# Dilated attention: softmax statistics of three groups joined over HBM instead of on TensorE

## The chip, the cores and the metric

The kernel runs on one NeuronCore of a Trainium2 chip. The metric is the device time of one execution in microseconds (us). Three executions of the kernel before took 3893.87 us in the median (3893.62 to 3896.42). A measurement of this kernel can tell a change of about 0.2% (some 8 us) from no change.

## The reference, cut to what matters

Two blocks of two layers each run over 512 tokens of width 1024, in float32. Only the last mixer, dilated attention in the second block, is touched. It has 16 heads of width 64 and three groups: group 0 with dilation 1, group 1 with dilation 4, group 2 with dilation 16. Each group has its own queries, keys and values. The three results are joined by their log-sum-exp:

```python
for g, (window, dilation) in enumerate(DIL_GROUPS):      # ((128, 1), (512, 4), (2048, 16))
    o, lse = strided_window_attention(q[g], k[g], v[g], dilation, window // dilation, rel_bias[g])
alpha = jax.nn.softmax(jnp.stack(lses, axis=0), axis=0)
o = jnp.sum(alpha[..., None] * jnp.stack(outs, axis=0), axis=0)
return o.reshape(B, S, DIL_WIDTH) @ w_o
```

For a token and a head that is one softmax over the keys of all three groups: the largest logit of the three is taken off before the exponential, and the three sums of exponentials are added.

## The kernel before, in words

All activations stay in SBUF with channels on the partitions and the 512 tokens on the free axis. Every linear layer is a chain of matmuls: a weight tile 128x128 is split into a high part `whi` and a low part `wlo`, the activations into `HH` and `HL`, and three matmuls (L409, L410, L411) make each product. The weights come from HBM in blocks of 8 tiles. SyncE (SP) loads a block 4 blocks ahead (`feed`, `load`), ScalarE (ACT) makes `whi`, VectorE (DVE) makes `wlo`. Each engine has its own program, written out by hand in order, and each wait is on a named signal. Nothing is rearranged by a scheduler.

The dilated stage (`dilated` in each engine's program) works in 8 rounds `c`, one for each pair of heads `hh_` = 0 and 1. A round has 9 steps. In step `n` TensorE (PE) first runs `head_proj(c + 1, n)`, the 24 matmuls of one of the nine projections (q, k, v of three groups) of the next pair, and after each v projection four transposes (L737). Then it runs `attend(c, n)`, a piece of the attention of this pair. The other engines run the same 9 steps: first their part of the projection, then their part of the attention. In the last round, `c` = 7, there is no projection left to put between the pieces.

The softmax statistics of a pair lie as columns: 12 tiles `s` (4 of each group) with 128 queries on the partitions, in `cm` (maxima), `cn` (negated joint maxima) and `cs` (sums). The queries of a tile are in the order of their group: in group 1 the tokens 4i + r, in group 2 the tokens of four residues of 16. To join the groups, their values must stand in token order. The pieces are:

- steps 0, 1: `logits`, q times k (L748 group 0, L755 group 1, L763 group 2). q and k lie in token order, so groups 1 and 2 are read with a stride of 4 or 16 elements. DVE adds the bias and takes the maxima (`biased`, L2032).
- step 2: `max_rows`, 12 matmuls turn the maxima to rows in token order (L777). DVE takes the maximum of three rows (`mrow`, L2043 to L2047).
- step 3: `max_cols`, 24 small matmuls turn the row back to 12 columns (L787, L790). DVE negates them (L2054).
- step 4, ACT only: `exps`, 24 exponentials with their sums, both heads (L1336).
- step 5: `sum_rows` adds the sums of the groups on PE (L798), DVE inverts them (L2060). Then `values` of head 0: 12 transposes of the exponentials (L808), ACT copies them to `PD` (`probs`, L1347), DVE spreads group 2 (`spread_probs`, L2067), PE multiplies by the values (L818, L824, L830).
- step 6: `values` of head 1.
- step 7: `spread` copies the inverse sums to 64 partitions each (L837), ACT takes them to `T[0]` (L1356), DVE multiplies (`finish`, L2073).

After round 7 comes the output projection `out_proj("dil")`, eight chains `m` of 24 matmuls. Each needs the results of all eight pairs, pair 7 at its end.

Of the kernel before, what the change touches and what calls it, by code (L numbers as in the profile page):

```python
# [16 lines left out]
S = 512  # L17
P = 128
# [81 lines left out]
def const_arrays():  # L100
# [11 lines left out]
    sel = np.zeros((P, P))  # L112
    sel[0, :64] = 1.0
    sel[1, 64:] = 1.0
    c["sel"] = sel
# [12 lines left out]
                ("band", 256), ("adiag", 4), ("sel", 128)]  # L128
# [76 lines left out]
def program(nc, xt, wst, mst, crow, vec, cst, trig, oh, tab, wax, out, bvec):  # L205
    with ExitStack() as ctx:
# [111 lines left out]
        mrow = at("mrow", cb_off + 2048, [2, S])  # L318
        cm = small[:, 64:88].rearrange("p (j h) -> p j h", h=2)
        cn = small[:, 88:112].rearrange("p (j h) -> p j h", h=2)  # L320
        cs = small[:, 112:136].rearrange("p (j h) -> p j h", h=2)
# [8 lines left out]
        def tok_view(ap, g, j):  # L330
            if g == 0:
                return ap[:, 128 * j:128 * j + 128]
            if g == 1:
                return ap.rearrange("p (i r) -> p r i", r=4)[:, j, :]
            return ap.rearrange("p (k a j) -> p j a k", k=32, a=4)[:, j, :, :]
# [19 lines left out]
            Signal(sem(n), 16) for n in ("vec_in", "cb_in", "wax_in", "oh_in", "tab_in", "trig_in", "fv_out", "x_out"))  # L355
        bb_in = [Signal(sem("bb_in%d" % i), 16) for i in range(2)]
# [3 lines left out]
        signals += x_in + [vec_in, cb_in, wax_in, oh_in, tab_in, trig_in, fv_out, x_out]  # L360

# [20 lines left out]
        def tensor_engine(lane):  # L382
# [341 lines left out]
            def dilated():  # L724
# [4 lines left out]
                def head_proj(c, n):  # L729
                    if c or n >= 4:  # L730
                        proj([("dl", c, n)], 8, hh, hl, ready)
                    g = n // 3
                    if n % 3 == 2:
                        o = take(("vt", c, g), main[0])
                        lane.wait_ge(a_mix, ("vt", c, g))
                        for j in range(4):
                            ins = e.transpose(o[:, 128 * j:128 * j + 128], tok_view(VT[:, g, :], g % 2, j), C["ident"][:])  # L737
                        ins.then_inc(*mm_done.up(("vt", c, g)))

                def logits(c, hh_):  # L740
# [19 lines left out]
                    for a_ in range(4):  # L760
                        for j in range(4):
                            r = 4 * a_ + j
                            ins = e.matmul(o[3][32 * j:32 * j + 32, 32 * a_:32 * a_ + 32], qk[hs, 4, r:S:16], qk[hs, 5, r:S:16],  # L763
                                           start=True, stop=True)
                    ins.then_inc(*mm_done.up(("lg", c, hh_, 3)))

                def row_view(o, g, j):
                    if g == 2:
                        return o.rearrange("p (i a j) -> p a j i", i=32, a=4)[:, j, :, :]
                    return tok_view(o, g, j)  # L770

                def max_rows(c):
                    o = take(("cm", c), pool_b)
                    lane.wait_ge(v_mix, ("lg", c, 1, 3))
                    for s in range(12):
                        g, j = s // 4, s % 4
                        ins = e.matmul(row_view(o[32 * g:32 * g + 2, :], g, j), cm[:, s, :], C["ident"][:], start=True, stop=True)  # L777
                    ins.then_inc(*mm_done.up(("cm", c)))

                def max_cols(c):  # L780
                    o = take(("cn", c), pool_b)
                    lane.wait_ge(v_mix, ("mrow", c))
                    for s in range(12):
                        g, j = s // 4, s % 4
                        at_ = o[:, 2 * s:2 * s + 2]
                        if g < 2:
                            e.matmul(at_, tok_view(mrow[:], g, j), C["ident"][0:2, 0:2], start=True, stop=True)  # L787
                            continue
                        for z in range(4):
                            ins = e.matmul(at_[32 * z:32 * z + 32, :], mrow[:, 4 * j + z:S:16], C["ident"][0:2, 0:2],  # L790
                                           start=True, stop=True)
                    ins.then_inc(*mm_done.up(("cn", c)))

                def sum_rows(c):
                    o = take(("cs", c), pool_b)
                    lane.wait_ge(a_mix, ("ex", c, 1))
                    for s in range(12):
                        ins = e.matmul(row_view(o[0:2, :], s // 4, s % 4), cs[:, s, :], C["ident"][:],  # L798
                                       start=s == 0, stop=s == 11, skip_group_check=True)
                    ins.then_inc(*mm_done.up(("cs", c)))  # L800

                def values(c, hh_):
# [26 lines left out]
                    for j in range(4):  # L829
                        ins = e.matmul(oh_.rearrange("p (i a j) -> p j a i", i=32, a=4)[:, j, :, :], vn[:, 8 + j, fs],  # L830
# [3 lines left out]
                def spread(c):  # L834
                    o = take(("sel", c), pool_b)
                    lane.wait_ge(v_mix, ("rc", c))
                    e.matmul(o, C["sel"][0:2, :], mrow[:], start=True, stop=True).then_inc(*mm_done.up(("sel", c)))  # L837
# [53 lines left out]
            lane.wait_ge(c_in["sel"], "in")  # L891
# [6 lines left out]
        def scalar_engine(lane):  # L898
# [406 lines left out]
            def dilated():  # L1305
                feed(8)

                def head_proj(c, n):
# [3 lines left out]
                    if n % 3 == 0:  # L1312
# [3 lines left out]
                        e.activation(QK[c % 2][:, 2 * g, :], bank(key), ACT.Copy, scale=0.125).then_inc(*a_mix.up(("dq", c, g)))  # L1316
                        freed[key] = ((a_mix, ("dq", c, g)),)
                    elif n % 3 == 2:
                        dst, src = VT[:, g, :], bank(key)
                        if g == 2:  # L1320
                            dst = dst.rearrange("p (j a k) -> p j a k", j=4, a=4)
                            src = src.rearrange("p (k a j) -> p j a k", k=32, a=4)
# [6 lines left out]
                def exps(c):  # L1329
                    lane.wait_ge(v_mix, ("cn", c))  # L1330
                    if c:
                        lane.wait_ge(mm_done, ("cs", c - 1))
                    for hh_ in range(2):
                        for s in range(12):
                            dst = SD[hh_][:, sd_at[s]:sd_at[s] + sd_wid[s]]
                            ins = e.activation(dst, dst, ACT.Exp, bias=cn[:, s, hh_:hh_ + 1], accum_out=cs[:, s, hh_:hh_ + 1])  # L1336
# [1142 lines left out]
```

## Time and profile before

| what | value |
|---|---|
| median of three runs | 3893.87 us |
| the profiled execution: its own time / its span | 3898.84 us / 3897.1 us |
| mean granted TensorE clock (1.00 is 2.4 GHz, 0.50 is 1.2 GHz) | 0.962 |
| PE busy / DVE busy / ACT busy | 3697.7 us (95%) / 2048.0 us (53%) / 1338.6 us (34%) |
| DMA share over the span | 31.0% of 16 engines |
| dilated stage, first logits to the last piece of round 7 | 2815.7 to 3455.9 us |

The trace gives each instruction's start and length. A busy PE row holds several matmuls, and neighbours overlap a little in it because matmuls are pipelined; a float32 matmul stands in it as two records. "Idle before" with an arrow names the instruction that ended the wait.

### The profile page before, as it was taken

To read this page: it belongs to the slowest core of one execution; us is meant where nothing else is said; L and a number is where in the kernel's file an instruction comes from. 1 tells how busy PE (TensorE), PEld (TensorE's weight loads), DVE (VectorE), ACT (ScalarE), POOL (GpSimd) and SP (SyncE) were. 2 spreads that over 40 slices of the span, in tenths; PEclk is the share of its full clock that TensorE was granted. 3 is DMA by queue.
4 is the path that set the end of the run, shared out by engine and by line. 5 is a ranking of instruction groups with operands and counts; after the bars stand their busy time and mean duration, and the time that the engine had idled before them with its cause. 6 is when DMAs were issued, how large, how long until landed. Compare 5 with 4: busy or idle time off the path is not lost.

```text
span 3897.1 us, 42188 instructions
## 1 busy us (share of the span) xinstructions
PE 3697.7 (95%) x17108; PEld 2932.7 (75%) x17108; DVE 2048.0 (53%) x3576; ACT 1338.6 (34%) x2299; POOL 127.9 (3%) x126
## 2 busy tenths in 40 slices
PE   6889999899999999988999999999999999989998
PEld 4647888666888788866678887888777777767886
DVE  7856756676756654466663246334533333345234
ACT  3563323443323322334432233223222322233222
POOL 2330000000000000001100000000000000000000
PEclk9999999989999999989999999999999999989999
DMA  6214555313555455311022222223211121112221
GB/s 243 97 44 164 203 185 189 140 56 119 185 202 189 170 195 193 110 66 38 20 78 98 97 98 81 98 93 100 82 59 59 59 65 63 55 44 87 96 94 65
DMA packets 125023, 426.58 MB, mean 109 GB/s; under 512 B 16107, under 2 KB 21099, under 8 KB 124828
## 3 DMA queue, kind: packets, MB, share of 16 engines
q1 hardware_dynamic: 124828, 423.88, 31.0%
q8 instruction: 135, 2.21, 0.2%
q14 instruction: 60, 0.49, 0.0%
HBM read 421.68 MB, written 2.14 MB: 109 GB/s over the span
## 4 chain that ended last, share of the span: by engine, by line
PE 84%; DVE 11%; ACT 3%; issue 1%; POOL 0%; ACTq 0%; DVEq 0%; POOLq 0%
PE ps L409 24%; PE ps L410 24%; PE ps L411 24%; PE ps L708 1%; PE ps L453 1%; PE ps L755 1%; PE ps L748 1%; PE ps L446 1%; DVE mrow L2060 1%; DVE TT L1522 1%; DVE HL L1507 1%; DVE wlo L1455 1%; PE ps L798 1%; PE ps L787 1%; DVE X L1608 1%
## 5 line engine op out<-in xcount | busy, mean ns | idle before, releaser
L409 PE MATMUL ps<-HH,whi 128*128 128x512 f32 x3168 | 1271.7, 401 | 45.3 <-DVE HL L1507 27.0
L410 PE MATMUL ps<-HL,whi 128*128 128x512 f32 x3168 | 1253.1, 396 | 0.0
L411 PE MATMUL ps<-HH,wlo 128*128 128x512 f32 x3168 | 1250.8, 395 | 0.0
L1455 DVE TENSOR_TENSOR wlo<-wraw,whi 128x1024 fp32r<-128x1024 f32 x526 | 643.8, 1224 | 692.0 <-ACT whi L920 691.8
L920 ACT ACTIVATE whi<-wraw 128x1024 fp32r<-128x1024 f32 x548 | 576.3, 1054 | 636.1 <-PE ps L411 624.2
L409 PEld LDWEIGHTS ps<-HH,whi 128*128 128x128 f32 x3168 | 607.0, 192 | 209.0 <-issue 67.2
L411 PEld LDWEIGHTS ps<-HH,wlo 128*128 128x128 f32 x3168 | 606.4, 191 | 130.4
L410 PEld LDWEIGHTS ps<-HL,whi 128*128 128x128 f32 x3168 | 607.2, 192 | 128.9 <-issue 4.6
L1443 DVE CUSTOM_DVE_ANT_0 mraw<-mraw,CB 128x1024 f32<-128x1024 f32 x224 | 282.3, 1261 | 0.8 <-DMA mraw<-mst 0.7
L1641 DVE TENSOR_TENSOR TT<-TT,ps 128x512 f32<-128x512 f32 x116 | 79.7, 687 | 217.2 <-PE ps L411 186.4
L409 PE MATMUL ps<-PHf,whi 128*128 128x512 f32 x352 | 136.9, 389 | 0.0
L410 PE MATMUL ps<-PLf,whi 128*128 128x512 f32 x352 | 136.9, 389 | 0.0
L409 PE MATMUL ps<-PHa,whi 128*128 128x512 f32 x352 | 136.9, 389 | 0.0
L410 PE MATMUL ps<-PLa,whi 128*128 128x512 f32 x352 | 136.9, 389 | 0.0
L409 PE MATMUL ps<-PHb,whi 128*128 128x512 f32 x352 | 136.9, 389 | 0.0
L410 PE MATMUL ps<-PLb,whi 128*128 128x512 f32 x352 | 136.9, 389 | 0.0
L411 PE MATMUL ps<-PHf,wlo 128*128 128x512 f32 x352 | 136.9, 389 | 0.0
L411 PE MATMUL ps<-PHa,wlo 128*128 128x512 f32 x352 | 136.9, 389 | 0.0
L411 PE MATMUL ps<-PHb,wlo 128*128 128x512 f32 x352 | 136.9, 389 | 0.0
L997 ACT ACTIVATE TT<-ps 128x512 f32<-128x512 f32 x72 | 42.9, 596 | 234.1 <-PE ps L411 234.1
L963 ACT ACTIVATE HH<-TT,MOD 128x512 fp32r<-128x512 f32 x63 | 45.2, 723 | 145.1 <-DVE TT L1522 145.1
L1336 ACT ACTIVATE SD<-SD,small 128x128 f32<-128x128 f32 (+1 forms) x192 | 74.1, 387 | 35.4 <-DVE small L2054 35.4
(329 smaller groups left out, 4012.5 us busy)
## 6 DMA issues: line engine op xcount, KB each, us to landing
wraw<-wst SPq DMA_DIRECT2D x548, 512.0 KB, 3.4
mraw<-mst SPq DMA_DIRECT2D x224, 512.0 KB, 3.4
MR<-mst SPq DMA_DIRECT2D x16, 512.0 KB, 13.8
X<-xt SPq DMA_DIRECT2D x8, 256.0 KB, 5.1
BB<-bvec SPq DMA_DIRECT2D x8, 256.0 KB, 3.7
out<-X SPq DMA_DIRECT2D x8, 256.0 KB, 2.0
CB<-crow SPq DMA_DIRECT2D x2, 512.0 KB, 4.3
BB<-bvec SPq DMA_DIRECT2D x8, 128.0 KB, 3.5
```

The source lines that it names most:

```text
L409: e.matmul(o[key], wh, sh(k), start=k == 0, stop=False)
L410: e.matmul(o[key], wh, sl(k), start=False, stop=False)
L411: ins = e.matmul(o[key], wl, sh(k), start=False, stop=k == nk - 1)
L446: ins = e.matmul(o[:, 4 * j + at_:4 * j + at_ + rhs.shape[1]], src[:, 128 * j:128 * j + 128], rhs, start=first and j == 0, stop=j == 3, sk ...
L453: e.matmul(o, C["ones"][:], T[0] if s[0] == "q" else T[2], start=True, stop=True).then_inc(*mm_done.up(("root", s)))
L920: e.activation(whi[:, b % SPLIT, :], wraw[:, b % RAW, :], ACT.Copy).then_inc(*whi_made.up(b))
L963: e.activation(HH[:, m, :], T[m % 5], ACT.Identity, bias=MOD[:, v, m:m + 1]).then_inc(*a_norm.up(("hh", s, m)))
L997: e.activation(a_, src, ACT.Silu).then_inc(*a_ffn.up(("silu", tag, i)))
L1336: ins = e.activation(dst, dst, ACT.Exp, bias=cn[:, s, hh_:hh_ + 1], accum_out=cs[:, s, hh_:hh_ + 1])
L1443: e.tensor_tensor_reduce(out=raw, in0=raw, in1=CB[:], scale=1.0, scalar=0.0, op0=ALU.mult, op1=ALU.add, accum_out=MOD[:, v, j:j + 1]).then ...
L1455: e.tensor_tensor(wlo[:, x % SPLIT, :], wraw[:, x % RAW, :], whi[:, x % SPLIT, :].bitcast(F32), ALU.subtract).then_inc(*wlo_made.up(x))
L1641: e.tensor_tensor(a_, a_, bank(("u", tag, i)), ALU.mult).then_inc(*v_ffn.up(("au", tag, i)))
```

## The change

The signals of the stage meet in HBM instead of on PE. A new DRAM tensor `lse` of 16 rows of 512 floats holds maxima, joint maxima, sums and inverses in token order. What changes:

- q, k and v of groups 1 and 2 are written to SBUF by residue (`by_residue`), so that the logits of these groups and the transposes of v read without a stride.
- The maxima of group 0 are turned to 8 rows by one matmul (`row_of`, key `mr`) and copied to `rows0`. Groups 1 and 2 go to HBM straight from their columns. SP's `maxima` issues 6 DMAs out, waits for them, and issues one that reads all six rows back with 4 tokens per partition (`lm`). DVE's `top` joins them. SP's `tops` writes the result, waits, and issues 5 DMAs that read it back, 4 of them straight to the columns of group 2. Group 0 comes back as rows and is turned by one matmul (`column_of`, key `tc`), for which PE waits in step 4 behind the signal `top_in`.
- The exponentials of head 0 move from step 4 to step 5 and those of head 1 to step 6. In step 6 they stand ahead of `probs` of head 0. `values` of head 0 moves from step 5 to 6, of head 1 from 6 to 7.
- The sums go the same way over HBM (`totals`, `invert`, `inverses`); the last DMAs write the inverses to 64 partitions each of `T[0]`. `finish` of a pair moves to step 1 of the next round. After round 7 SP runs `totals(7)` and `inverses(7)` ahead of the weight loads that follow.

```diff
-                    elif step == 2:
-                        max_rows(c)
-                    elif step == 3:
-                        max_cols(c)
-                    elif step == 5:
-                        sum_rows(c)
+                    elif step == 2:
+                        row_of(("mr", c), cm[:, 0, :, :], v_mix, ("lg", c, 1, 3))
+                    elif step == 4:
+                        column_of(c)
+                    elif step == 6:
                         take(("od", c), ob)
                         values(c, 0)
-                    elif step == 6:
+                    elif step == 7:
                         values(c, 1)
-                    elif step == 7:
-                        spread(c)
+                        row_of(("sr", c), cs[:, 0, :, :], a_mix, ("ex", c, 1))
...
+                def row_of(key, columns, signal, name):
+                    o = take(key, pool_b)
+                    lane.wait_ge(signal, name)
+                    e.matmul(o[0:8, 0:128], columns.rearrange("p h j -> p (h j)"), C["ident"][:], start=True, stop=True).then_inc(
+                        *mm_done.up(key))
+
+                def column_of(c):
+                    o = take(("tc", c), pool_b)
+                    lane.wait_ge(top_in, (c, 0))
+                    e.matmul(o[:, 0:8], rows0[:, 1, :], C["ident"][0:8, 0:8], start=True, stop=True).then_inc(*mm_done.up(("tc", c)))
...
                     for r in range(4):
-                        ins = e.matmul(o[2][:, 128 * r:128 * r + 128], tok_view(qk[hs, 2, :], 1, r), tok_view(qk[hs, 3, :], 1, r),
-                                       start=True, stop=True)
+                        rs = slice(128 * r, 128 * r + 128)
+                        ins = e.matmul(o[2][:, rs], qk[hs, 2, rs], qk[hs, 3, rs], start=True, stop=True)
...
-                        if step == 4:
-                            exps(c)
-                        elif step in (5, 6):
-                            probs(c, step - 5)
-                        elif step == 7:
-                            spread(c)
+                        if step in (5, 6):
+                            exps(c, step - 5)
+                        if step in (6, 7):
+                            probs(c, step - 6)
...
+                def top(c):
+                    lane.wait_ge(max_in, c)
...
+                    m = cn[:, 1, :, :]
+                    e.tensor_tensor(m, lm[:, 0, :, :], lm[:, 1, :, :], ALU.max).then_inc(*v_mix.up(("top0", c)))
+                    lane.wait_ge(v_mix, ("top0", c))
+                    e.tensor_tensor(m, m, lm[:, 2, :, :], ALU.max).then_inc(*v_mix.up(("top1", c)))
+                    lane.wait_ge(v_mix, ("top1", c))
+                    e.tensor_scalar(m, m, -1.0, None, ALU.mult).then_inc(*v_mix.up(("top", c)))
...
+                def maxima(c):
+                    lane.wait_ge(v_mix, ("mr", c))
...
+                    for tile, offset, strides in orders(cm, 0, 2048):
+                        e.dma_start(place(0, offset, strides), tile).then_inc(*max_out.up(c))
+                    lane.wait_ge(max_out, c)
...
+                    e.dma_start(flat(lm), rows(0, 6)).then_inc(*max_in.up(c))
+
+                def tops(c):
+                    lane.wait_ge(v_mix, ("top", c))
...
+                    e.dma_start(rows(6, 2), cn[:, 1, :, :]).then_inc(*top_out.up(c))
+                    lane.wait_ge(top_out, c)
+                    for tile, offset, strides in orders(cn, 1, 0):
+                        if offset < 1024:
+                            e.dma_start(tile, place(6, offset, strides)).then_inc(*top_in.up((c, 0), (c, 2)))
...
+                for c in range(8):
+                    if c < 7:
+                        bias_in(c + 1)
+                    for n in range(9):
+                        if c < 7:
+                            feed(8)
+                        if n == 1 and c:
+                            totals(c - 1)
+                        elif n == 2 and c:
+                            inverses(c - 1)
+                        elif n == 5:
+                            maxima(c)
+                        elif n == 6:
+                            tops(c)
+                totals(7)
+                inverses(7)
```

ACT's program in round 0, from the v projection of step 5 on. In the kernel before, `SD_154` and `SD_155` are the logits and exponentials of heads 0 and 1:

```order
1379 L1336 ACTIVATE SD_154,small<-SD_154,small 128x128 [waits v_mix]
...
1383 L1336 ACTIVATE SD_155,small<-SD_155,small 128x128
...
1386 L1336 ACTIVATE SD_155,small<-SD_155,small 128x32 x4
1387 L920 ACTIVATE whi<-wraw 128x1024 [waits mm_done,w_in3]
1388 L1326 ACTIVATE VT<-ps 128x512 [waits mm_done]
1389 L1347 ACTIVATE PD<-ps 128x512 [waits mm_done] x2
1390 L1347 ACTIVATE PD<-ps 128x384 [waits mm_done]
1391 L920 ACTIVATE whi<-wraw 128x1024 [waits w_in4]
1392 L1316 ACTIVATE QK_150<-ps 128x512 [waits mm_done]
1393 L1347 ACTIVATE PD<-ps 128x512 [waits mm_done] x2
```

The same place in the changed kernel, where the two heads are `SD_153` and `SD_154`:

```order
1380 L1295 ACTIVATE VT<-ps 128x512 [waits mm_done]
1381 L1306 ACTIVATE SD_153,small<-SD_153,small 128x128 [waits top_in,v_mix]
...
1384 L1306 ACTIVATE SD_153,small<-SD_153,small 128x32 x4
1385 L891 ACTIVATE whi<-wraw 128x1024 [waits w_in4]
1386 L1288 ACTIVATE QK_149<-ps 128x512 [waits mm_done]
1387 L1306 ACTIVATE SD_154,small<-SD_154,small 128x128
1388 L1306 ACTIVATE SD_154,small<-SD_154,small 128x256 x3
...
1390 L1306 ACTIVATE SD_154,small<-SD_154,small 128x32 x4
1391 L1317 ACTIVATE PD<-ps 128x512 [waits mm_done] x2
1392 L1317 ACTIVATE PD<-ps 128x384 [waits mm_done]
```

The 12 exponentials of the second head have moved behind the evacuation of the projection of step 6 and ahead of the first head's `PD` copies.

SP's program in round 0 of the changed kernel. `rows_159` is `rows0`, `small` holds the columns. Before, these rows were only `wraw` loads:

```order
467 L2222 DMA wraw<-wst 128x1024 [waits wlo_made] x6
468 L2276 DMA lse<-rows_159 8x128 [waits v_mix]
469 L2276 DMA lse<-small 128x2x4
470 L2276 DMA lse<-small 32x2x4 x4
471 L2280 DMA small<-lse 128x6x4 [waits max_out]
472 L2222 DMA wraw<-wst 128x1024 [waits wlo_made]
473 L2288 DMA lse<-small 128x2x4 [waits v_mix]
474 L2292 DMA rows_159<-lse 8x128 [waits top_out]
475 L2292 DMA small<-lse 32x2x4 x4
476 L2222 DMA wraw<-wst 128x1024 [waits wlo_made] x2
```

Four transfers now follow one another between the maxima and the exponentials, and one weight load stands between them.

PE's program in round 0 of the changed kernel at the end of steps 2 and 4; 24 projection matmuls of step 3 and 24 of step 4 lie between the two small ones:

```order
10585 L740 MATMUL ps<-c_ident,VT 128x128 x3
10586 L805 MATMUL ps<-c_ident,small 8x128 [waits v_mix]
10587 L412 MATMUL ps<-HH,whi 128x512 [waits wlo_made]
...
10634 L414 MATMUL ps<-HH,wlo 128x512
10635 L811 MATMUL ps<-c_ident,rows_159 128x8 [waits top_in]
10636 L412 MATMUL ps<-HH,whi 128x512 [waits v_mix,wlo_made]
```

The wait for `top_in` stands in PE's program ahead of the projection of step 5.

## Rows read from the trace of the kernel before

**Rows 1.** The page, chain of waits that ended last, share by engine.
```profile
PE 84%; DVE 11%; ACT 3%; issue 1%; POOL 0%; ACTq 0%; DVEq 0%; POOLq 0%
```

**Rows 2.** Waits, 2740 to 3460 us: who waited for whom, total us, times, longest.
```profile
PE ps L737 <- ACT VT L1326: 17.2, 23, 0.8
```

**Rows 3.** Timeline of PE, round 3: start us, length us, line, out<-in, records.
```profile
3074.31 2.02 PE L755 MATMUL ps<-QK 64*128 64x128 f32 x8
...
3094.17 1.92 PE L777 MATMUL ps<-c_ident,small 128*2 128x128 f32 x24
3101.68 2.91 PE L787 MATMUL ps<-c_ident,mrow 2*128 2x2 f32 x16
3104.53 0.66 PE L790 MATMUL ps<-c_ident,mrow 2*32 2x2 f32 x32
...
3119.31 2.78 PE L798 MATMUL ps<-c_ident,small 128*2 128x128 f32 x24
3122.03 1.53 PE L808 MATMUL ps<-c_ident,SD 128*128 128x128 f32 x12
...
3125.07 1.04 PE L824 MATMUL ps<-PD,VN 128*64 128x128 f32 x8
...
3133.10 1.47 PE L808 MATMUL ps<-c_ident,SD 128*128 128x128 f32 x12
3134.50 1.74 PE L818 MATMUL ps<-PD,VN 128*64 128x128 f32 x14
...
3143.62 1.12 PE L837 MATMUL ps<-mrow,c_sel 2*128 2x512 f32 x2
```

**Rows 4.** Timeline of ACT, the same round.
```profile
3105.47 0.40 ACT L1336 ACTIVATE SD<-SD,small 128x128 f32<-128x128 f32 x1 [2.14 <-DVE small L2054]
...
3110.11 0.39 ACT L1336 ACTIVATE SD<-SD,small 128x128 f32<-128x128 f32 x1
...
3122.72 1.47 ACT L1347 ACTIVATE PD<-ps 128x512 f32<-128x512 f32 x3 [4.20 <-PE ps L808]
...
3133.30 0.60 ACT L1316 ACTIVATE QK<-ps 128x512 f32<-128x512 f32 x1 [8.17 <-PE ps L411]
```

**Rows 5.** DMA issues: out<-in, count, KB each, median us from issue to landing.
```profile
out<-X SPq DMA_DIRECT2D x8, 256.0 KB, 2.0
...
BB<-bvec SPq DMA_DIRECT2D x32, 8.0 KB, 2.9
...
bvec<-FV SPq DMA_DIRECT2D x1, 44.0 KB, 1.7
```

**Rows 6.** Timeline of SP's queue: six issues in a row.
```profile
3117.43 2.86 SPq L2273 DMA_DIRECT2D BB<-bvec  x6
```

**Rows 7.** DMA queue, 3288 to 3294 us: packets, MB, share of 16 engines.
```profile
q1 hardware_dynamic: 988, 0.95, 51.1%
```

**Rows 8.** The same for 3298 to 3304 us, one weight block alone.
```profile
q1 hardware_dynamic: 144, 0.52, 26.4%
```

**Rows 9.** Stretches: length, PE busy (records), granted clock, DMA share, GB/s.
```profile
2906.00:2908.00 2.00, 2.00 (x5) 0.50 0.00 0
...
3104.00:3108.00 4.00, 4.00 (x44) 0.79 0.11 22
3108.00:3112.00 4.00, 4.00 (x15) 0.79 0.27 110
...
1746.20:1751.20 5.00, 5.00 (x12) 0.50 0.00 0
```

**Rows 10.** Timeline of PE at that last stretch: idle before in brackets.
```profile
1746.18 0.77 PE L428 MATMUL ps<-whi,CH 128*128 128x512 f32 x1 [5.09 <-DVE CW L1721]
```

**Rows 11.** Timeline of PE, round 7.
```profile
3408.63 1.78 PE L748 MATMUL ps<-QK 64*128 64x128 f32 x8
...
3454.76 1.12 PE L837 MATMUL ps<-mrow,c_sel 2*128 2x512 f32 x2
```

**Rows 12.** Timeline of DVE, round 7: the negated maxima are ready.
```profile
3429.74 0.18 DVE L2054 TENSOR_SCALAR small<-ps 128x24 f32<-128x24 f32 x1 [3.04 <-PE ps L790]
```

More of the change, by code:

```diff
@@ L317, in program @@
         RB = at("RB", cb_off, [P, 4, 4, 32])
[L318 to L321, printed above, removed]
+        cm, cn, cs, lm, ls = (small[:, a:a + 24].rearrange("p (g h j) -> p g h j", g=3, h=2) for a in (64, 88, 112, 136, 0))
+        inverse = small[:, 24:32].rearrange("p (h j) -> p h j", h=2)
+        rows0 = at("rows0", cb_off + 2048, [8, 3, P])
         def col(name, i=0, w=1):
@@ L772, in max_rows @@
[L772 to L800, printed above, removed]
+                    for b in range(4):
+                        for r in range(4):
+                            at_ = 32 * (4 * b + r)
+                            ins = e.matmul(o[3][32 * b:32 * b + 32, 32 * r:32 * r + 32], qk[hs, 4, at_:at_ + 32],
+                                           qk[hs, 5, at_:at_ + 32], start=True, stop=True)
@@ L890, in tensor_engine @@
             post_norm(1, 0)
-            lane.wait_ge(c_in["sel"], "in")
             dilated()
@@ L1327, in head_proj, with exps @@
                         freed[key] = ((a_mix, ("vt", c, g)),)
-                def exps(c):
-                    lane.wait_ge(v_mix, ("cn", c))
+                def exps(c, hh_):
+                    lane.wait_ge(v_mix, ("tc", c))
+                    lane.wait_ge(top_in, (c, 2))
                     if c:
[L1332 to L1336, printed above, removed]
-                        ins.then_inc(*a_mix.up(("ex", c, hh_)))
+                        lane.wait_ge(sum_out, c - 1)
+                        lane.wait_ge(mm_done, ("sr", c - 1))
+                    for s in range(12):
+                        g, j, dst = s // 4, s % 4, SD[hh_][:, sd_at[s]:sd_at[s] + sd_wid[s]]
+                        ins = e.activation(dst, dst, ACT.Exp, bias=cn[:, g, hh_, j:j + 1], accum_out=cs[:, g, hh_, j:j + 1])
+                    ins.then_inc(*a_mix.up(("ex", c, hh_)))
                 def probs(c, hh_):
@@ L2089, in dilated @@
                         elif step == 2:
-                            max_rows(c)
+                            row_out(("mr", c), 0, max_out)
                         elif step == 3:
-                            max_cols(c)
-                        elif step == 5:
-                            sum_rows(c)
+                            top(c)
+                        elif step == 4:
+                            column_in(c)
+                        elif step == 6:
                             spread_probs(c, 0)
-                        elif step == 6:
+                        elif step == 7:
                             spread_probs(c, 1)
-                        elif step == 7:
-                            finish(c)
+                            row_out(("sr", c), 2, sum_out)
+                        elif step == 8:
+                            invert(c)
+                        if step == 1 and c:
+                            finish(c - 1)
+                finish(7)
                 keep(7)
@@ L2273, in bias_in, with orders, place @@
                             e.dma_start(BB[c % 2][np_ * z:np_ * z + np_, :, to:to + nk], view).then_inc(*bb_in[c % 2].up(c))
+                def orders(tile, row0, g2_row):
+                    yield rows0[:, row0, :], 0, [[128, 8], [1, 128]]
+                    yield tile[:, 1, :, :], 1024, [[4, P], [512, 2], [1, 4]]
+                    for n in range(4):
+                        yield tile[32 * n:32 * n + 32, 2, :, :], g2_row + 4 * n, [[16, 32], [512, 2], [1, 4]]
+                def place(row, offset, strides):
+                    return bass.AP(lse.tensor, lse.offset + 512 * row + offset, strides)
@@ new lines, in inverses @@
+                def inverses(c):
+                    lane.wait_ge(v_mix, ("inv", c))
+                    if c:
+                        lane.wait_ge(inv_in, c - 1)
+                        lane.wait_ge(v_mix, ("yf", c - 1))
+                    e.dma_start(rows(14, 2), inverse).then_inc(*inv_out.up(c))
+                    lane.wait_ge(inv_out, c)
+                    for h in range(2):
+                        e.dma_start(T[0][64 * h:64 * h + 64, :], place(14 + h, 0, [[0, 64], [1, 512]])).then_inc(*inv_in.up(c))
@@ L2275, in dilated @@
                 bias_in(0)
                 feed(40)
-                for c in range(1, 8):
-                    bias_in(c)
-                    feed(72)
+                for c in range(8):
[12 more added lines that the diff above has]
+                            tops(c)
```

128 lines of the change are left out of this document (69 added, 59 removed).

## The prediction

> **What bounds the kernel now.** I read the page first, then the waits of the dilated stage, then the timelines of PE, ACT and SP in one round, then the granted clock in short stretches. The chain of waits that ended last runs on PE for 84% of the span [rows 1]. In the dilated stage the longest single wait of PE in rounds 0 to 6 is 0.8 us, for the copy of v ahead of its transposes [rows 2]. So PE is never really idle there: every matmul taken out of a round is worth its time, and every wait put in costs its time. ACT and DVE have slack of 8 us and more at several places of a round (the bracket of 8.17 in [rows 4]), but their order matters, since PE waits for what stands in a queue behind something else.
>
> A second thing counts. After short, thin matmuls the granted clock falls to 0.50 (1.2 GHz of 2.4) for about 3.4 us: 0.79 over the 8 us behind L787 and L790 [rows 9] is 3.4 us at half clock, which costs 1.7 us of PE. It happens in each of the rounds 0 to 6 there, and behind the logits in six of the seven, as at 2906 us [rows 9].
>
> **What the change takes from PE, per round.** max_rows 1.92, max_cols 2.91 + 0.66, sum_rows 2.78, spread 1.12: 9.4 us [rows 3]. It adds two single matmuls of the form that L777 and L798 had twelve of (0.16 and 0.23) and one of the eight of L787 (0.36): 0.75. The logits of group 1 had eight records in 2.02; eight records of the same columns without stride stand at L824 with 1.04: 0.98 saved for each head, 1.96. That is 10.6; rows overlap their neighbours by some 0.07 each (L808 starts 2.71 after L798, not 2.78), so I take **10.2** (9.5 to 10.6). The half clock behind max_cols goes with its cause: **1.7** more. That behind the logits may go as well, now that they are denser: 0 to 1.7, taken as **0.5**, since nothing in the rows says that the stride caused it. The strided copies to `QK` and `VT` I cost at nothing: v of group 2 was already copied with a stride of 16 and took the same 0.60 as the others, and PE's wait of 0.8 [rows 2] stays.
>
> **First new wait: `top_in` at the end of step 4.** From the end of matmul `mr` in step 2 PE has two projection groups before it asks for `top_in`. One is 5.6 us (L777 ends at 3096.1, L787 starts at 3101.68 [rows 3]), together **11.2**. In that time this must happen, one after the other:
> - DVE's copy of v (0.69 long) and of the row: 0.7.
> - Six issues on SP. Six take 2.86 us [rows 6], so the sixth starts 2.4 after the first. Its landing isn't shown for writes of 16-byte pieces. Bounds: 1.9, near the two writes to HBM that there are (1.7 and 2.0 [rows 5]), and 3.2, the small reads of 64 pieces (2.9 [rows 5]) and a little for more pieces. 4.3 to 5.6.
> - The read of six rows in 768 pieces of 16 bytes. In 6 us with a weight block and six bias transfers the engines worked 51.1% of their time, with the block alone 26.4% [rows 7, 8]: 23.7 engine-us for 844 packets, 28 ns each. 704 pieces more than in the small reads are 704 x 28 ns / 16 = 1.2 us on top of 2.9. 3.5 to 4.3.
> - Three small DVE operations of 0.18 [rows 12] with their handoffs: 0.8.
> - The write of the result: 1.9 to 3.4.
> - Five issues, the fifth 1.9 after the first, landing 2.9 later [rows 5, 6]: 4.8 to 5.0.
> - Four handoffs between engines, 0.1 each: 0.4.
>
> The sum is 16.4 to 20.2, less 11.2 is 5.2 to 9.0, and up to 1 more where a small transfer queues behind the 512 KB weight block that SP issues in between. I take **7.2** of stall, near the landings of the small reads. Behind the waiting PE stands the projection of step 5, so all of it counts. DVE waits in `top` too, ahead of its `wlo` of two groups later; that is 11 us away and harmless. SP's weight loads wait behind these DMAs, but they run four blocks (22 us) ahead, which hides it.
>
> **Second new wait: `PD` in step 6.** In the changed order ACT must evacuate the projection of step 6 before it can start the 12 exponentials of head 1, and only then come head 0's `PD` copies, for which PE's `values` wait right after their transposes. In the trace that evacuation starts at 3133.30 and holds ACT for 0.5; 12 exponentials take 4.64 (3105.47 to 3110.11) [rows 4]; from the start of the `PD` copies to the first product 0.77 passes (3122.72 [rows 4] to 3123.49, where the transposes end: 3122.03 + 1.53 [rows 3] less the overlap). So the first product could start at 3133.30 + 0.5 + 4.64 + 0.77 = 3139.2, where before it started at 3134.50 [rows 3]: 4.7 late. A wait of 0.4 for `RB` in the old step 5, behind the 3.35 us reciprocal, goes. **4.3** (4.0 to 5.0). Nothing hides it: the exponentials can't start earlier, since ACT's evacuation waits for the very group that PE ends just ahead of `values`.
>
> **What each stall does to the clock.** After an idle of 5.09 us [rows 10] PE ran 5.0 us at 0.50 [rows 9]. The stalls here are as long, so each costs half of such a stretch, **2.5** (1.4 to 3), as it falls on dense matmuls.
>
> **Round and stage.** -10.2 - 1.7 - 0.5 + 7.2 + 2.5 + 4.3 + 2.5 = +4.1 us, in seven rounds +29. Low ends: -10.6 - 1.7 - 1.7 + 5.2 + 1.4 + 4.0 + 1.4 = -2.0, -14. High ends: -9.5 - 1.7 + 10 + 3 + 5 + 3 = +9.8, +69.
>
> **Round 7** has no projections to hide anything. Before, from its first logits (3408.63 [rows 11]) 21.3 us pass to the exponentials (3429.9 [rows 12]) and 26 more to the end of PE's work (3454.76 + 1.12 [rows 11]); one group of the output projection (5.5) follows at once. After: logits and their maxima 11.9 as before, `finish` and `keep` of earlier pairs and the row 1.9, the chain above without its first 0.7, 15.7 to 19.5, and 0.7 for turning the column: 30.2 to 34.0, so 9 to 12.6 later. From there two heads of exponentials, copies and products without sum_rows and spread: 18.8, 7 less than before. Then the sums: row 0.3, six issues 4.3 to 5.6, read 3.5 to 4.3, DVE 0.8, write 1.9 to 3.4, two broadcasts of 128 KB 4.2, handoffs 0.4, then finish, high and low part and the last matmuls 3.3: 18.7 to 22.3, against the 5.5 of the output group, which can hide all but its last product: 13.2 to 16.8 more, less the 7. Together +15 to +22, and 2.5 for the half clock behind the idle: **+20** (17 to 25).
>
> Sum: +29 + 20 = **+49 us**. The profiled execution took 3898.8 (span 3897.1), 5.0 over the median of the runs; its successor should take 3948, and the median goes from 3893.9 to **3943 us**. Ends: 3893.9 - 14 + 17 = 3897, and 3893.9 + 69 + 25 = 3988.
>
> **Rivals.**
> - All transfers land in 2.0 us, whatever their pieces, as `out<-X` does [rows 5]. The four landings are then 8 us and the chain 8 + 2.4 + 1.9 + 0.7 + 0.8 + 0.4 = 14.2, the stall 3.0, 4.2 less in each round (-29) and 8 less in round 7: 3906. For it: both writes in the trace. Against it: the small reads at 2.9, with less to move than `out<-X`. Chance 0.14. (The Trainium skill, "DMA: Bandwidth & Descriptors", section "Anatomy of one DMA", gives a fixed cost of about 2.0 us per DMA, most of it the write receipt; the trace agrees for the large writes only. By its figure the sum would be this rival's.)
> - Faster: the round trip hides under the two projection groups. With a stall under 2 us the clock need not fall either (-2.5), so a round loses 10.2 + 1.7 + 0.5 and pays only 4.3 + 2.5: -5.6, seven times -39, round 7 +12: 3867. It decides from where the chain is under some 13 us, a mean landing under 1.7 us, the fastest in [rows 5]. Chance 0.06.
> - The clock doesn't fall behind the stalls: 5.0 less per round, 3908. Against it: [rows 9, 10]. Chance 0.08.
> - 16-byte pieces are slow to write, hops of 5 us: the stall is 8 longer in each round, 16 in round 7: 4015. No row has such pieces. Chance 0.10.
> - The stride of 4 was not what made L755 slow: +14, 3957, inside the forecast's range.
> - The forecast: chance 0.62.
>
> **How the numbers follow.** The range 3905 to 3990 takes in the forecast's own ends nearly whole, the 2.0 us case and the unmoved clock; outside are the slow pieces and the hidden round trip. 0.2% (8 us) is what a measurement can tell. Faster: the hidden round trip and a sliver of the low ends, 0.07. Same: low edges of the first and third rival and of the forecast, 0.09. Slower 0.84.
>
> **What would show it.** In the changed profile PE's small `tc` matmul waits for a DMA of `rows0` or `small` some 7 us in each round; the first product of head 0 waits 4 to 5 us for ACT's `PD`; the clock is 0.50 for some 5 us behind both; L755's eight records take 1.0 us; the output projection starts, then waits some 15 us for pair 7. The forecast is wrong if the `tc` wait is under 2 us, if `PD` isn't late in step 6, or if PE waits elsewhere, for weights above all.

## The result, and the profile after

The changed kernel took 3871.72 us (median, 3867.95 to 3879.0), the kernel before 3895.14 beside it on the same chip: a ratio of 0.9937 (0.9925 to 0.995), 23.4 us or 0.6% faster. The forecast was 3943, slower. The profiled execution had a span of 3876.9 us (3897.1 before) at a mean granted clock of 0.960 (0.962).

The page, line of busy times and chain of waits that ended last. PE still leads the chain, with 81% for the 84% of [rows 1], but DMA and SP's queue, absent before, now hold 3%:

```profile
PE 3619.1 (93%) x16372; PEld 2876.8 (74%) x16372; DVE 2017.1 (52%) x3608; ACT 1333.8 (34%) x2291; POOL 128.0 (3%) x126
...
PE 81%; DVE 11%; ACT 4%; DMA 2%; issue 1%; SPq 1%; POOL 0%; ACTq 0%; DVEq 0%; POOLq 0%
```

Waits of PE from 2800 to 3450 us (who waited for whom: total us, times, longest). The third row is that of [rows 2]; the others are new. The 22.9 us of the second are 12.0 in round 7 and 10.9 in rounds 0 to 6, 1.56 for each:

```profile
PE ps L786 <- ACT PD L1317: 34.0, 8, 4.5
PE ps L811 <- DMA small<-lse: 22.9, 8, 12.0
PE ps L740 <- ACT VT L1295: 16.5, 22, 0.8
PE ps L412 <- DVE HL L1682: 9.8, 1, 9.8
PE ps L776 <- ACT SD L1306: 5.1, 1, 5.1
```

Timeline of PE, round 3 and the piece of round 0 in which the maxima travel (start us, length us, line, out<-in, records, in brackets the idle time before and its releaser). The logits of group 1 (L759, which was L755) take 1.05 instead of 2.02; `mr` (L805) and `tc` (L811) stand for the thin matmuls of [rows 3]. From the start of `mr` to that of `tc` 12.5 us pass in round 0 and 14.7 in round 3, whose wait of 3.21 is the longest of the seven. The first product L786 starts 4.46 late:

```profile
2838.97 0.38 PE L805 MATMUL ps<-c_ident,small 128*8 128x128 f32 x2
...
2851.49 0.38 PE L811 MATMUL ps<-c_ident,rows 8*128 8x8 f32 x2 [1.03 <-DMA small<-lse]
...
3067.21 1.78 PE L751 MATMUL ps<-QK 64*128 64x128 f32 x8
3068.83 1.05 PE L759 MATMUL ps<-QK 64*128 64x128 f32 x8
...
3077.71 0.38 PE L805 MATMUL ps<-c_ident,small 128*8 128x128 f32 x2
...
3092.41 0.59 PE L811 MATMUL ps<-c_ident,rows 8*128 8x8 f32 x2 [3.21 <-DMA small<-lse]
...
3114.01 3.25 PE L786 MATMUL ps<-PD,VN 128*64 128x128 f32 x14 [4.46 <-ACT PD L1317]
3117.05 1.91 PE L792 MATMUL ps<-PD,VN 128*64 128x128 f32 x8
```

SP's queue over the maxima of round 0 (start us, length of the issues, x for their number). Six writes, the last issued near 2842.2; the read of six rows at 2843.66; the write of the result at 2846.33; its broadcast from 2847.95:

```profile
2839.99 0.30 SPq L2276 DMA_DIRECT2D lse<-rows  x1
2840.33 2.30 SPq L2276 DMA_DIRECT2D lse<-small  x5
2843.66 0.38 SPq L2280 DMA_DIRECT2D small<-lse  x1
2844.08 0.54 SPq L2222 DMA_DIRECT2D wraw<-wst  x1
2846.33 0.36 SPq L2288 DMA_DIRECT2D lse<-small  x1
2847.95 0.29 SPq L2292 DMA_DIRECT2D rows<-lse  x1
2848.28 1.72 SPq L2292 DMA_DIRECT2D small<-lse  x4
```

So the hops (from the issue of a transfer to what waits for its landing) took 1.5 us (last write to read), 1.9 (read to the next write, less 0.75 for three DVE operations), 1.6 (write) and 1.9 (last broadcast, issued at 2849.6, to `tc`). The list of DMA issues from 2800 to 3450 us has the medians (KB each, median us to landing), the read of 768 pieces of 16 bytes included; single writes of the result took 1.5 to 2.4:

```profile
TT<-lse SPq DMA_DIRECT2D x16, 128.0 KB, 3.0
...
lse<-small SPq DMA_DIRECT2D x32, 4.0 KB, 1.9
...
BB<-bvec SPq DMA_DIRECT2D x24, 8.0 KB, 2.7
...
small<-lse SPq DMA_DIRECT2D x16, 12.0 KB, 2.0
```

Stretches of round 3 (length, busy time with records of PE, PEld, DVE, ACT and POOL, granted clock, DMA share, GB/s), behind the `tc` wait, around the `PD` wait and behind it; the last stretch lies behind the logits of round 1, where the clock had fallen to 0.50 before in six of seven rounds [rows 9]:

```profile
3092.40:3099.00 6.60, 6.59 (x17) 5.28 (x18) 1.30 (x2) 0.00 (x0) 0.00 (x0) 0.53 0.70 220
3105.00:3112.00 7.00, 4.55 (x27) 3.71 (x25) 1.23 (x1) 6.26 (x27) 0.00 (x0) 1.00 0.23 75
3112.00:3119.00 7.00, 4.99 (x24) 4.99 (x25) 2.26 (x5) 3.76 (x14) 0.00 (x0) 0.52 0.12 33
...
2900.95:2904.00 3.05, 3.05 (x43) 2.63 (x43) 2.52 (x17) 0.00 (x0) 0.00 (x0) 1.00 0.00 0
```

One thing in the logits got slower, and the forecast had it at nothing. The 16 small products of group 2 are issued in another order: before, each writes another block of 32 partitions than the one ahead of it; now four in a row write the same block. The rows of one head, before, after, in the kernel before with dense q and k, and in the changed kernel with strided ones (both kernels are told below):

```profile
3412.20 0.84 PE L763 MATMUL ps<-QK 64*32 64x32 f32 x32
3069.81 0.90 PE L766 MATMUL ps<-QK 64*32 64x32 f32 x32
3308.12 0.46 PE L770 MATMUL ps<-QK 64*32 64x32 f32 x32
3339.78 1.42 PE L767 MATMUL ps<-QK 64*32 64x32 f32 x32
```

In the old order these products take 0.84 strided and 0.46 dense, in the new order 1.42 and 0.90. The changed kernel so gives back, by the rows, 0.44 for each head, 6.2 us in rounds 0 to 6. No run exchanges the order alone.

The account in stages, read off PE's timelines (a round is from head 0's first logits to those of the next; the tail from round 7's first logits to the first evacuation of the output projection):

| kernel | rounds 0 to 6 | tail | both, against before |
|---|---|---|---|
| before | 592.9 | 53.0 | |
| after | 560.5 | 61.8 | -23.6 |
| q and k by residue alone | 566.7 | 50.4 | -28.8 |
| after, q and k in token order | 585.5 | 64.2 | +3.8 |
| after, one more trip over HBM | 587.7 | 62.3 | +4.1 |
| after, `probs` first | 509.7 | 58.8 | -77.4 |
| and the maxima one step later | 499.1 | 58.4 | -88.4 |
| that, one more trip over HBM | 499.4 | 58.6 | -87.9 |

A round of after is 4.6 us shorter than one of before, where the forecast had it 4.1 longer.

### The profile page after: what moved, and what is told of

It is laid out like the page before. It is cut to its first block, busy times and chain, and to the rows that moved or that the text cites. A ratio compares the mean times of both kernels' runs of the same rounds, so it can differ in the third digit from the quotient of the medians.

```text
span 3876.9 us, 40995 instructions
## 1 busy us (share of the span) xinstructions
PE 3619.1 (93%) x16372; PEld 2876.8 (74%) x16372; DVE 2017.1 (52%) x3608; ACT 1333.8 (34%) x2291; POOL 128.0 (3%) x126
## 4 chain that ended last, share of the span: by engine, by line
PE 81%; DVE 11%; ACT 4%; DMA 2%; issue 1%; SPq 1%; POOL 0%; ACTq 0%; DVEq 0%; POOLq 0%
PE ps L412 23%; PE ps L414 23%; PE ps L413 23%; ACT SD L1306 1%; PE ps L786 1%; PE ps L711 1%; DMA lse<-small 1%; DMA small<-lse 1%; PE ps L456 1%; PE ps L449 1%; DVE TT L1483 1%; DVE HL L1468 1%; DVE wlo L1416 1%; PE ps L751 1%; DVE X L1569 1%
## 5 line engine op out<-in xcount | busy, mean ns | idle before, releaser
L412 PE MATMUL ps<-HH,whi 128*128 128x512 f32 x3168 | 1264.9, 399 | 58.9 <-DVE HL L1468 28.1
L412 PEld LDWEIGHTS ps<-HH,whi 128*128 128x128 f32 x3168 | 603.0, 190 | 216.7 <-issue 63.3
L412 PE MATMUL ps<-PHf,whi 128*128 128x512 f32 x352 | 136.9, 389 | 0.0
L412 PE MATMUL ps<-PHa,whi 128*128 128x512 f32 x352 | 136.9, 389 | 0.0
L412 PE MATMUL ps<-PHb,whi 128*128 128x512 f32 x352 | 136.9, 389 | 0.0
L1977 DVE COPY VN<-ps 128x512 f32<-128x512 f32 x24 | 16.6, 692 | 128.4 <-PE ps L740 128.4
## 6 DMA issues: line engine op xcount, KB each, us to landing
MR<-mst SPq DMA_DIRECT2D x16, 512.0 KB, 13.6
```

The costliest lines, as they stand in the source:

```text
L412: e.matmul(o[key], wh, sh(k), start=k == 0, stop=False)
```

## The experiments

The trace of after says that the round trip is short, and that no half clock is left behind the logits. The theory was that the stride of q and k had been the cause of that half clock, so that the dense logits carry the gain while the two waits eat what the thin matmuls gave; the rival, that the clock is set by what else stands near the logits.

**Strided logits put back.** All of the change stays, but q and k lie in token order again (the edit, shortened):

```diff
-  ins = e.matmul(o[2][:, rs], qk[hs, 2, rs], qk[hs, 3, rs], start=True, stop=True)
+  ins = e.matmul(o[2][:, rs], tok_view(qk[hs, 2, :], 1, r), tok_view(qk[hs, 3, :], 1, r),
+                 start=True, stop=True)
...
-  at_ = 32 * (4 * b + r)          # then qk[hs, 4, at_:at_ + 32], qk[hs, 5, at_:at_ + 32]
+  at_ = 4 * b + r                 # then qk[hs, 4, at_:S:16], qk[hs, 5, at_:S:16]
```

> The changed kernel, but q and k of groups 1 and 2 stay in token order and the logits read them with strides of 4 and 16 elements, as before the change. Theory: the strided reads cost twice 0.97 us per round (eight records in 2.02 instead of 1.05) and bring back the half clock behind the logits (1.7 us in six of seven rounds): +3.4 us per round, +24 in seven, +2 in round 7, so about 3897 us, as fast as the kernel before; the statistics over HBM alone then bring nothing. Rival: the half clock behind the logits went with the small matmuls of the statistics and stays away; only 2 x 0.97 x 8 = +15 us, 3887.

Measured 3905.5 us, 1.0022 (1.0009 to 1.0034) of before, 34 above after by the medians; on the traces the seven rounds are 25.0 longer than after's. So +15 is too little. The theory's +26 fits the traces, but not by its own terms: 13.6 us are group 1 (L759), 7.3 are group 2 (1.42 instead of 0.90 for each head), which it had left out, and some 4 are left for the clock. The 8 us above before are no verdict on the trip over HBM: the same products take 1.42 here and 0.84 there, with the same strides, which is 8.1 us in seven rounds. The half clock behind the logits is back in four rounds of the seven (0, 3, 4 and 5), not in six, as in round 0 (same columns as above):

```profile
2820.00:2827.00 7.00, 7.00 (x47) 5.56 (x47) 2.60 (x17) 0.00 (x0) 0.00 (x0) 0.51 0.23 75
```

**The dense logits alone.** The kernel before, with q and k of groups 1 and 2 written by residue, the logits reading them without a stride, and nothing else; group 2 keeps the old order of its products. The edit at q, shortened (the same at k):

```diff
-  e.activation(QK[c % 2][:, 2 * g, :], bank(key), ACT.Copy, scale=0.125)
+  dst, src = by_residue(QK[c % 2][:, 2 * g, :], g)[0], by_residue(bank(key), g)[1]
+  e.activation(dst, src, ACT.Copy, scale=0.125)
```

> The kernel before with one part of the change: q and k of groups 1 and 2 are written by residue and the logits read without a stride; the statistics still go over TensorE. Theory: -24 to -26 us, about 3870, the whole gain of the change; the granted clock no longer falls behind the logits but still does behind L787 and L790. Rival: the gain is that of the matmuls taken off TensorE, and this part alone brings 15 us or less (3879 or more).

Measured 3868.42, 0.9928 (0.9917 to 0.994), 29 us faster than before and level with after (0.9925 to 0.995). As much as the whole change gained lies in this part; the rest of the change gains 6.2 in the rounds on top (566.7 to 560.5), with the 6.2 lost by the order of group 2's products in it, and loses 11.4 in the tail. The clock is 1.00 over a piece of round 1 with and behind its logits, and still falls behind the thin matmuls of `max_cols`, which this kernel keeps:

```profile
2896.80:2905.00 8.20, 8.20 (x72) 6.96 (x72) 3.94 (x25) 1.54 (x2) 0.00 (x0) 1.00 0.19 66
2926.00:2930.00 4.00, 4.00 (x41) 3.25 (x42) 1.32 (x2) 3.14 (x15) 0.00 (x0) 0.62 0.25 62
```

**`probs` ahead of `exps` in ACT's step.** After, with two statements exchanged, so that head 0's `PD` copies don't stand behind head 1's exponentials:

```diff
+  if step in (6, 7):
+      probs(c, step - 6)
   if step in (5, 6):
       exps(c, step - 5)
-  if step in (6, 7):
-      probs(c, step - 6)
```

> The changed kernel with two entries of ScalarE's step 6 swapped: the PD copies of head 0 stand ahead of the exponentials of head 1. Theory: the 4.46 us wait of the first product (L786) goes in each of seven rounds, and with it most of the half clock behind it (2.3 us of TensorE per round), and some 3 us in round 7: about -50 us against the changed kernel, 3822. Rival: the exponentials of head 1 are then late for its transposes in step 7 and the wait turns up there: no gain, 3872.

Measured 3820.76, 0.9803 (0.979 to 0.9816): 51 us faster than after. A wait of 4.46 us, taken out of each of seven rounds, gave back 7.3 in each. The L786 row is gone from PE's waits (2800 to 3300 us), and the 14 records of `values`' first products (L786), which had 3.25 at half clock, run in 1.74, with nothing idle before them:

```profile
PE ps L740 <- ACT VT L1295: 15.8, 21, 0.8
PE ps L811 <- DMA small<-lse: 10.4, 7, 2.9
```
```profile
3079.95 1.47 PE L776 MATMUL ps<-c_ident,SD 128*128 128x128 f32 x12
3081.35 1.74 PE L786 MATMUL ps<-PD,VN 128*64 128x128 f32 x14
```

**The turned maxima one step later.** The kernel just told, with `column_of` on PE and `column_in` on DVE in step 5, so that a third projection group lies over the trip:

```diff
-  elif step == 4:
+  elif step == 5:
       column_of(c)        # and the same for column_in(c) on DVE
```

> As e3_probs_first, and besides the small matmul that waits for the joint maxima (tc) and its copy stand at the end of step 5 instead of step 4, so that three projection groups lie over the HBM round trip instead of two. Theory: the wait for the round trip (0.9 to 3.2 us per round, 1.6 in the mean) goes; the exponentials of head 0 then have one projection group, 5.5 us, for 4.7 us of work and become a wait of up to 0.5 us: -1 to -2 us per round against e3_probs_first, about 3812. Rival: the exponentials of head 0 are late by the whole evacuation behind them, and it is no faster or some us slower than e3_probs_first.

Measured 3812.96, 0.9782 (0.9769 to 0.9795). The rounds are 1.5 us shorter each, which is the size of the `tc` wait of the run before (1.49 in the mean); it has left the list (2800 to 3300 us):

```profile
PE ps L740 <- ACT VT L1295: 15.8, 21, 0.8
PE ps L786 <- ACT PD L1317: 1.5, 7, 0.2
```

This version is the fastest: 2.2% under before, 1.5% under after.

**One more trip over HBM.** After, with the read of the six rows made twice, one landing ahead of the other:

```diff
+  e.dma_start(flat(lm), rows(0, 6)).then_inc(*max_in.up(("first", c)))
+  lane.wait_ge(max_in, ("first", c))
   e.dma_start(flat(lm), rows(0, 6)).then_inc(*max_in.up(c))
```

> The changed kernel with one more transfer in the chain of the maxima: SP waits for the read of the six rows and issues the same read again. Theory: one such hop costs 2.0 to 2.3 us (issue to landing 2.0 for 12 KB in the changed kernel's trace), all of it stall, since the round trip already ends 1.6 us late; in some rounds the granted clock falls too (1.7 us each): +2 to +4 us in each of eight rounds, +16 to +32, about 3895. Rival, as in the forecast: small transfers cost 2.9 to 4.1 us each and the chain is short for another reason; then the second read alone adds 4 us in each round, +35 and more.

Measured 3901.54, 1.0011 (1.0002 to 1.0019), 30 above after by the medians; on the traces 3.9 in each round: 2.0 of wait (the total without round 7's 14.4 is 24.7, 3.5 in each round for 1.56) and 1.9 of half clock. So a hop is 2.0 us, not the forecast's 3.5 to 4.3 for this read; the theory holds, and the rival that wanted 35 or more falls. Waits of PE, and the landing of that read, 2800 to 3450 us:

```profile
PE ps L811 <- DMA small<-lse: 39.1, 8, 14.4
```
```profile
small<-lse SPq DMA_DIRECT2D x24, 12.0 KB, 2.0
```

**The same trip in the fastest version.**

> e5_late_column with the same extra transfer. Theory: the chain (12.3 us, 14.4 with the extra hop) lies under three projection groups (16.8 us), so seven rounds pay nothing and only round 7, which has no projections, pays 2.1 us and some half clock: +2 to +4 us, 3816. Rival: the transfer costs something by occupying SP, the DMA engines or HBM, whatever lies over it: +15 us and more, as in e4_extra_hop.

Measured 3810.45, 0.9776 (0.9762 to 0.979), the same as without it; the rounds differ by 0.3 us in all. Only round 7 waits longer (14.4). The same trip cost 30 us a moment ago and costs nothing here: its price is set by the work of PE that lies over the trip, not by the transfer.

**Why the small reads of the row had 2.9 us.** Two runs, with one time each, ask where the forecast's dearest number came from. First the kernel before with the three bias transfers of a block in reverse order, 8 KB ahead of 128 and 256 KB:

> The kernel before, with the bias transfers of a round issued in the other order: the four of 8 KB first, then 128 KB, then 256 KB. Theory: the 2.9 us from issue to landing that the forecast took for a small transfer were spent in a queue behind the 384 KB issued just ahead; issued first, the small ones land in 1.5 to 2.2 us. Rival: a read of many short pieces lands in 2.9 us by itself, and it stays 2.7 to 3.1. The time of the kernel is 3894 to 3898 us by both.

The 8 KB landed in 2.6 us instead of 2.9, the time was 3898.21. The expected 1.5 to 2.2 was missed: the 384 KB of the same round's biases account for 0.3 only. Then the same, with SP waiting ahead of them until the 512 KB weight block issued before had landed:

> As e6_small_first, and SP waits until the weight block issued just before (512 KB) has landed, so that nothing lies ahead of the four 8 KB transfers. Theory: in e6_small_first they landed in 2.6 us because that block was still moving; alone they land in 1.5 to 2.0 us, as the small transfers of the changed kernel do. Rival: reads of bvec are slow by their form (64 pieces of 128 bytes that overlap), and they stay at 2.6 us. The kernel's time stays within 3891 to 3900 us by both.

```profile
BB<-bvec SPq DMA_DIRECT2D x32, 8.0 KB, 2.6
```
```profile
BB<-bvec SPq DMA_DIRECT2D x32, 8.0 KB, 1.8
```

The first row is of the first kernel, the second of the second: 1.8 us when nothing lay ahead in SP's queue, and 3895.14 for the kernel. The form of the read isn't slow; it stood behind 512 KB.

## Why the prediction was wrong, step by step

The sign was wrong, though each of the mechanisms named was there. Per round of 0 to 6, forecast and measured:

| term | forecast | measured |
|---|---|---|
| matmuls taken out, dense logits | -10.2 | -9.9 |
| half clock behind `max_cols` | -1.7 | -1.7 |
| half clock behind the logits | -0.5 | -1.5 |
| `tc` waits for the maxima | +7.2 | +1.6 |
| half clock behind that | +2.5 | +0.7 |
| `PD` late in step 6 | +4.3 | +4.1 |
| half clock behind that | +2.5 | +2.3 |
| sum | +4.1 | -4.4 (round: -4.6) |

The first row is read from start to start: 9.05 for the matmuls that went, less 0.95 for the three that came, 1.94 for group 1 (0.97 for each head, 0.98 forecast), less 0.13 for group 2. That last term the forecast had at nothing: 0.38 for each head gained by dense operands and 0.44 lost by the new order. The half-clock rows are counted from the clock of each stretch: before it fell 13 times for 3.4 us (7 behind `max_cols`, 6 behind the logits), after in 9 stretches of 3.4 or 6.8 us with 41.3 us of busy PE, of which 31.7 behind the `PD` wait, 9.6 behind the `tc` wait and none behind the logits; half of each is taken as lost. For the logits that is the most it can be: the rows of L763 are as long at half clock (0.84) as at full (0.82). The `PD` wait is 4.46 less the 0.4 for `RB` that went.

**The step that failed is the chain of landings behind `top_in`.** The forecast added up 16.4 to 20.2 us for it and took a stall of 7.2, "near the landings of the small reads", the 2.9 of [rows 5]. Measured in round 0 it is 12.3, from the end of `mr` (2839.2) to `tc` (2851.5), against the 11.2 of the two projection groups over it. By terms, forecast and measured: six writes 4.3 to 5.6, 3.7; read 3.5 to 4.3, 1.9; write of the result 1.9 to 3.4, 1.6; five broadcasts 4.8 to 5.0, 3.5. The `tc` wait came to 1.56 for 7.2; the forecast itself had named a wait under 2 us as a sign that it is wrong. The cause is one: the 2.9 was read off transfers that the same queue had put behind 896 KB, and 1.2 more was added for 16-byte pieces. In the changed kernel the hops took 1.5 to 1.9, and the read of 768 pieces landed in 2.0, where one of 64 with an empty queue had 1.8. The low end of the landings, 1.7 and 2.0 for two writes, stood in the same rows and was the right end. The Trainium skill ("DMA: Bandwidth & Descriptors", section "Anatomy of one DMA") gives about 2.0 us of fixed cost for a DMA, worked out there for those that GpSimd issues. That was nearer than the forecast's price: here, issued by SP, the read landed in 2.0 and the writes in 1.9 in the median. Even the rival worked out with 2.0 for every landing (stall 3.0, 3906 us, chance 0.14) was too slow: its chain had 14.2 us for 12.3, and it kept the two errors that follow. The rival that came nearest was the hidden round trip (3867, chance 0.06): it set the turning point at a chain of 13 us and a mean landing of 1.7, where the runs have 12.3 and 1.5 to 1.9.

**A stall was charged the clock whatever its length.** The forecast took 2.5 us of half clock behind each, from an idle time of 5.09 [rows 10]. Behind the 4.46 it came in every round. Behind the `tc` waits (1.03, 1.62, 0.91, 3.21, 1.06, 1.36, 1.75) it came in rounds 3 and 6 alone. This is also why a hop of 2.0 us cost 3.9 in after: it made them 2.64 to 5.51 us long, and the clock fell behind all seven. Where it begins to fall isn't shown: a wait of 1.75 brought it here, one of 1.72 in the run with `probs` first didn't.

**The stride was called unproved, and was the cause.** "Nothing in the rows says that the stride caused it": the two experiments on the logits do. In rounds 0 to 6 the clock falls behind the logits of strided q and k in six rounds of seven before and in four of seven with the rest of the change; behind dense ones it falls in none of the 42 rounds of the six kernels that have them. Why some rounds with strides keep the clock is not shown. The fall that went gives at most 1.0 a round more than taken, 7 us.

**Round 7** was to pay 20 and paid 8.9. From its first logits to the exponentials 23.5 us pass where 30.2 to 34.0 were expected (the `tc` wait is there in full):

```profile
3379.89 1.78 PE L751 MATMUL ps<-QK 64*128 64x128 f32 x8
...
3390.01 0.59 PE L805 MATMUL ps<-c_ident,small 128*8 128x128 f32 x2 [0.72 <-DVE small L1995]
3402.56 0.59 PE L811 MATMUL ps<-c_ident,rows 8*128 8x8 f32 x2 [11.97 <-DMA small<-lse]
3408.26 2.79 PE L776 MATMUL ps<-c_ident,SD 128*128 128x128 f32 x12 [5.10 <-ACT SD L1306]
...
3424.84 0.39 PE L805 MATMUL ps<-c_ident,small 128*8 128x128 f32 x2
3440.04 0.80 PE L412 MATMUL ps<-HH,whi 128*128 128x512 f32 x1 [9.79 <-DVE HL L1682]
```

Of the 6.7 us below the forecast's low end 4.4 are the chain of maxima (11.3 from the copied row, whose copy ends at 3391.25 on DVE, to `tc`, forecast 15.7 to 19.5) and 2.4 lie ahead of it: 11.4 from the first logits to that copy, forecast 13.8, since `mr` starts after 10.1 where 11.9 had been taken over from before. The chain of the sums, L805 to L412, is 15.2 for 18.7 to 22.3. In both chains the error is the landings again. Against before, the exponentials come 2.2 later (9 to 12.6 forecast), the heads' products end 4.2 sooner (7 forecast: they run at half clock behind the waits), and the output projection waits 10.8 more (13.2 to 16.8).

**What was right:** the `PD` wait in place, cause (ACT's queue, in order, behind an evacuation that PE itself releases) and size; the weight of a thin matmul; that `VT`'s 0.8 us wait stays [rows 2] (16.5 and 17.2 in all); that SP's weight loads don't run short. The range left even the forecast's own low end (3897) outside, and the chance of a faster kernel, 0.07, was hung on the fastest landing in the rows, while the slowest had been priced in without asking what stood ahead of it.

**Why round 3 waits longest.** Its read is issued 5.8 us after the first of the six writes, for 3.7 in round 0 (3078.72 and 3084.49 in SP's queue). From the last write to the read 3.3 to 3.6 us pass there in every kernel with the trip, and 1.4 to 1.8 in all 15 other such trips of maxima and sums. In these six cases, and in no other of the 96, the trace has a packet of 16 KB of the kind `instruction` that starts 1.1 to 1.3 us after the last write. In the changed kernel it runs from 3082.04 for 1.17 us, and eight of the writes' pieces of 16 bytes move only behind it, at 3083.2 to 3083.3. From 3082.0 to 3083.1 us (queue, kind: packets, MB, share):

```profile
q8 instruction: 1, 0.02, 6.6%
q1 hardware_dynamic: 7, 0.00, 0.3%
```

That is some 1.2 of the 2.1 us; where the rest goes stays open, and no experiment moved the packet.

## What to carry to other kernels

Price a small transfer from one that had nothing ahead of it in its queue; the median landing of a list mixes in the queue, and here it turned the sign. A stall costs its length, and the half clock behind it if it is long; it costs nothing if one more group of other work lies over it. So look first at the order in the queue of the engine that is waited for: two exchanged statements were worth 51 us here, twice the change itself. And run a change's parts alone: the layout of q and k by itself brought as much as all of this one, and a new order of 16 small products, which nobody had priced, took 6 us back.

## What the runs showed of the hardware

- PE was busy without a gap through the logits of rounds 0 to 6, and yet the granted clock fell to 0.50 behind strided operands of 64 rows (0.51 over 7.00 us in the run with strides), in 10 rounds of 14, and stayed at 1.00 behind dense ones in 42 of 42. Four float32 matmuls of 64 x 128 on 128 columns (eight records) took 2.02 us with a stride of 4 and 1.05 without.
- Sixteen float32 matmuls of 64 x 32 on 32 columns took 0.46 us (dense) and 0.84 (stride of 16) when each wrote another block of 32 partitions than the one before, and 0.90 and 1.42 when four in a row wrote the same block.
- Waits of 0.91 to 1.62 us left the clock alone in five rounds of the changed kernel, and one of 1.72 in the run with `probs` first; those of 1.75, 3.21 and 4.46 brought 3.4 or 6.8 us at half clock.
- A read of 12 KB in 768 pieces of 16 bytes landed in 2.0 us, a write of 4 KB to HBM in 1.5 to 2.4 (median 1.9), and an 8 KB read in 1.8 with an empty queue, 2.6 behind a 512 KB block and 2.9 behind 896 KB.
